# First mixer's query, key and gate projections as seven block products per weight half, with weight sums made beside them

## What is computed

```python
proj = h @ w_in                                  # (512, 1024) @ (1024, 4096)
q, k, v, gate = jnp.split(proj, 4, axis=-1)
...
sc = jnp.einsum('bhqd,bhqnd->bhqn', qb, kg).astype(jnp.float32) * scale
sc = sc + bb.astype(jnp.float32)[None]           # neighbourhood bias, 16 heads
pr = jax.nn.softmax(sc, axis=-1).astype(vg.dtype)
...
return (o * jax.nn.silu(gate)) @ w_out
```

## Time and profile before

| what | us |
|---|---|
| three runs | 1194.61, 1192.61, 1194.82; median 1194.61 |
| profiled execution, device time | 1197.42 |
| span of its trace | 1195.6 |
| busy in the span: PE, DVE, ACT, POOL | 1135.7, 592.3, 507.3, 416.0 |

### The profile page before, as it was taken

How to read it: one execution, slowest core, us unless ns; L and a number is a source line. 1 busy time by engine, 2 the same in 40 slices (tenths; PEclk the granted TensorE clock), 3 DMA queues, 4 the chain that set the end, 5 groups by cost and what they waited for, 6 DMA issues and landing times.

```text
span 1195.6 us, 24300 instructions
## 1 busy us (share of the span) xinstructions
PE 1135.7 (95%) x10103; PEld 952.0 (80%) x10103; DVE 592.3 (50%) x1312; ACT 507.3 (42%) x1025; POOL 416.0 (35%) x363
## 2 busy tenths in 40 slices
PE   3999999999999999899999999988999999999996
PEld 3998888799998998656699998966777887677763
DVE  5000001762427247788623338127875887445656
ACT  4232222973424432488833355243883531122211
POOL 4734574776335445300253334230015341000000
PEclk9999999999999999999999999989999899999999
DMA  7432342323221223200042223342002222100001
GB/s 218 147 98 79 106 115 97 98 69 85 72 86 56 93 85 106 71 1 2 4 139 72 72 71 128 124 137 71 2 2 71 71 91 98 55 27 3 4 2 70
DMA packets 73335, 89.57 MB, mean 75 GB/s; under 512 B 2017, under 2 KB 66666, under 8 KB 73098
## 3 DMA queue, kind: packets, MB, share of 16 engines
q1 hardware_dynamic: 70136, 78.12, 20.3%
q0 software_dynamic: 2416, 8.26, 2.8%
q10 hardware_dynamic: 674, 1.64, 0.5%
HBM read 83.75 MB, written 4.26 MB: 74 GB/s over the span
## 4 chain that ended last, share of the span: by engine, by line
PE 83%; DVE 7%; ACT 5%; POOL 2%; issue 2%; ACTq 1%; DMA 0%; DVEq 0%; POOLq 0%
PE bank L477 77%; PE bank L804 2%; ACT arena L1378 2%; POOL ring_parts L2697 2%; PE bank L714 1%; PE bank L1003 1%; ACT ring_parts L1407 1%; PE bank L569 1%; ACT arena L1494 1%; ACT arena L1759 1%; ACTq L1373 1%; DVE arena L2420 0%; ACT arena L1387 0%; DMA ring<-in_cmp_w_v 0%; POOL arena_parts L2703 0%
## 5 line engine op out<-in xcount | busy, mean ns | idle before, releaser
L2697 POOL TENSOR_TENSOR ring_parts<-ring,ring_parts 128x512 fp32r<-128x512 f32 (+1 forms) x236 | 307.7, 1337 | 435.7 <-ACT ring_parts L1407 344.0
L477 PE MATMUL bank<-ring_parts,arena_parts 128*128 128x256 f32 x1856 | 322.8, 283 | 0.0
L477 PEld LDWEIGHTS bank<-ring_parts,arena_parts 128*128 128x128 f32 x1856 | 272.2, 190 | 2.0 <-DVE stat L2245 1.2
L477 PE MATMUL bank<-hT_parts,ring_parts 128*128 128x512 f32 x704 | 235.2, 396 | 0.0
L477 PE MATMUL bank<-arena_parts,ring_parts 128*128 128x512 f32 x640 | 225.3, 402 | 2.8 <-POOL ring_parts L2697 2.8
L477 PE MATMUL bank<-ring_parts,hT_parts 128*128 128x256 f32 x1024 | 222.9, 285 | 3.8 <-POOL ring_parts L2697 2.9
L1378 ACT ACTIVATE arena<-bank 128x512 f32<-128x512 f32 (+5 forms) x287 | 135.2, 540 | 195.3 <-PE bank L477 191.4
L477 PEld LDWEIGHTS bank<-ring_parts,hT_parts 128*128 128x128 f32 x1024 | 172.2, 192 | 5.0 <-POOL ring_parts L2697 3.7
L477 PE MATMUL bank<-arena 64*64 64x64 f32 (+7 forms) x1904 | 163.0, 316 | 6.8 <-ACT arena L1759 2.3
L477 PEld LDWEIGHTS bank<-hT_parts,ring_parts 128*128 128x128 f32 x704 | 133.4, 190 | 31.3
L477 PEld LDWEIGHTS bank<-arena_parts,ring_parts 128*128 128x128 f32 x640 | 122.9, 192 | 32.1 <-ACT arena L1378 3.0
(11 more groups left out here) (271 smaller groups left out, 1406.5 us busy)
## 6 DMA issues: line engine op xcount, KB each, us to landing
ring<-in_a_w_in SPq DMA_DIRECT2D x16, 1024.0 KB, 5.5
ring<-in_w_in SPq DMA_DIRECT2D x15, 1024.0 KB, 5.5
ring<-in_b_w_in SPq DMA_DIRECT2D x10, 1024.0 KB, 5.0
ring<-in_ple_w_gate SPq DMA_DIRECT2D x8, 1024.0 KB, 5.2
...
```

The costliest lines, as they stand in the source:

```text
L477: return nc.tensor.matmul(o, l, r, start=start, stop=stop)
L2697: nc.gpsimd.tensor_tensor(rounded(r), r, read_back(high_slot(n)[:, o:o + m // 4]), ALU.subtract)\
```

## The change

The four values halves stay as they are. For the twelve others (`SEVEN`, h = 0 to 11) the product is cut into 2 x 2 x 2 blocks (512 rows of k, 128 output features, 256 tokens) and made of seven block products instead of eight, with sums of weight blocks on the left and sums of token blocks on the right.

- **TensorE.** A product (`seventh`, number m = 7h + q) is 4 k x 3 matmuls with 256 moving columns. Products q = 4, 5, 6 go on in banks that hold q = 0, 3, 1, once these have been read.
- **Operands.** Six double places of 128x512 (`operand`, `NOP` = 6) take the weight operands, high and low; they lie in the fourth raw slot and both high slots, and the raw halves turn over three slots. ScalarE writes the high part (`high_operand`), GpSimd the low part of q = 0, 1, 2, 3, 6, VectorE that of q = 4, 5. VectorE makes the four weight sums of a half (`sum_operand`). Operands are prepared five products ahead and wait for the product that frees their place.
- **Tokens.** VectorE makes three sums of token blocks of 128x1024 and one in place, and their low parts, during the values halves. They lie in `x` and in the arena; SyncE loads `x` again behind `AO` 3.
- **Results.** ScalarE copies the first product; VectorE adds the others to it (`second_out`, `third_out`, `last_out`); ScalarE reads the block of q = 4 (`left_out`). Gates: tanh from the copied gate, then `gate_a` on VectorE from two tiles in SBUF.
- **GpSimd.** All low parts of operands stand before head 4's bias. The four quarters of `AO` 0 stand before the biases of heads 8 to 11, those of `AO` 1 before heads 12 to 15. Two small DMAs into `wa` move behind the attention, since `wa` holds a weight sum.

The core of the diff:

```diff
-        AORD = list(range(8, 12)) + list(range(8)) + list(range(12, 16))
+        SEVEN = list(range(8)) + list(range(12, 16))
+        AORD = list(range(8, 12)) + SEVEN
         for n in AORD:
-            half(("A", n), A["a_w_in"][0], n)
...
+        def operand(m):
+            o = HALF * NRAW7 + 2 * 4 * P * ((m + 2) % NOP)
+            return quarter(ring[:, o:o + 4 * P]), quarter(ring[:, o + 4 * P:o + 8 * P])
+        s2_sum = quarter(wa[:, :])
+        h_full, h_low = (v["norm0"].rearrange("p (k t) -> p k t", k=KB) for v in (full, low))
+        x4 = x[:, :, :].rearrange("p i d -> p (i d)")
+        T1, T2, T4 = ((quarter(x4[:, 0:1024]), quarter(x4[:, 3072:4096])),
+                      (quarter(x4[:, 1024:2048]), quarter(area(16384, 1024))),
+                      (quarter(x4[:, 2048:3072]), quarter(area(17408, 1024))))
+        def tokens_of(kh, th):
+            return block4(hT[:, :, :], kh, th, 256), block4(h_low, kh, th, 256)
+        T3 = tokens_of(0, 1)
+        RIGHT = [tokens_of(0, 0), T1, T2, T3, tokens_of(1, 0), T4, tokens_of(1, 1)]
+        def source(m):
+            h, q = divmod(m, 7)
+            return {0: weight_block(h, 0, 0), 1: weight_block(h, 0, 1), 2: s2_sum, 4: weight_block(h, 1, 0),
...
+        LAST_OF = ("1", "6", "6", "7", "11", "21", "12")
+        def free_operand(eng, m):
+            if m < 2:
+                eng.wait_ge(filled, half_last[2] + 1)
+            elif m < NOP:
+                eng.wait_ge(filled, half_last[3] + 1)
+            else:
+                h, q = divmod(m - NOP, 7)
+                eng.wait_ge(filled, J[("A", SEVEN[h], LAST_OF[q])] + 1)
...
+            def seventh(m, b, again=False):
+                h, q = divmod(m, 7)
+                if q in (4, 5):
+                    pe.wait_ge(S("A_low_v"), 2 * h + q - 3)
                 else:
-                    for s in range(2):
-                        fm3(("A", n, s), "a" if n < 8 else "v", ("A", n), s * P, act)
-                used3(("A", n))
+                    pe.wait_ge(S("A_low_g"), 5 * h + min(q, 4) + 1)
+                left, right = (tuple(rounded(v) for v in pair) for pair in (operand(m), RIGHT[q]))
+                def one(a, c, k, st, sp):
+                    return nc.tensor.matmul(b[:, 0:256], left[a][:, k, :], right[c][:, k, :], start=st, stop=sp,
+                                            skip_group_check=again)
+                for k in range(4):
+                    one(0, 0, k, k == 0 and not again, False)
+                    one(0, 1, k, False, False)
+                    ins = one(1, 0, k, False, k == 3)
+                return ins
+            pe.wait_ge(S("A_tlow"), 3)
+            for h, n in enumerate(SEVEN):
+                m = 7 * h
+                b1 = begin(("A", n, "11"), "a", apart=True)
+                also(("A", n, "1"), ("A", n, "11"), "a")
+                end(seventh(m, b1), ("A", n, "1"))
+                b5 = begin(("A", n, "12"), "v", apart=True)
+                seventh(m + 1, b5)
+                b6 = begin(("A", n, "6"), "v", apart=True)
+                end(seventh(m + 2, b6), ("A", n, "6"))
+                b7 = begin(("A", n, "21"), "v", apart=True)
+                also(("A", n, "7"), ("A", n, "21"), "v")
+                if h == 0:
+                    pe.wait_ge(S("A_tlow3"), 1)
+                end(seventh(m + 3, b7), ("A", n, "7"))
+                evacuated(pe, ("A", n, "1"))
+                end(seventh(m + 4, b1, True), ("A", n, "11"))
+                evacuated(pe, ("A", n, "7"))
+                end(seventh(m + 5, b7, True), ("A", n, "21"))
+                pe.wait_ge(S("A_22"), h + 1)
+                end(seventh(m + 6, b5, True), ("A", n, "12"))
...
+            def high_operand(m):
+                h, q = divmod(m, 7)
+                if q in (1, 2, 3, 6):
+                    act.wait_ge(S("A_sum"), 4 * h + min(q, 4))
+                else:
+                    raw_here(act, first7 + h)
+                free_operand(act, m)
+                nc.scalar.activation(rounded(operand(m)[0]), source(m), ACT.Copy).then_inc(S("A_high"), 1)
...
+            def h_block(kh, t):
+                return block4(h_full, kh, t, 256)
+            evacuated(dve, ("norm0", 3, 1))
+            dve.wait_ge(s_wlo, 8)
+            TT(T1[1], h_block(0, 1), h_block(0, 0), ALU.subtract).then_inc(S("A_tsum"), 1)
+            dve.wait_ge(S("A_tsum"), 1)
+            TT(T2[1], h_block(1, 1), T1[1], ALU.subtract).then_inc(S("A_tsum"), 1)
+            dve.wait_ge(S("A_tsum"), 2)
+            TT(T4[1], h_block(1, 0), T2[1], ALU.subtract).then_inc(S("A_tsum"), 1)
+            dve.wait_ge(S("lo_norm0"), 8)
+            TT(h_block(0, 1), h_block(1, 1), h_block(0, 1), ALU.subtract).then_inc(S("A_tsum"), 1)
+            for n, t in enumerate((T1, T2, T4)):
+                dve.wait_ge(S("A_thigh"), n + 1)
...
+            def sum_operand(m):
+                h, q = divmod(m, 7)
+                if q == 1:
+                    raw_here(dve, first7 + h)
+                    s1 = weight_block(h, 0, 1)
+                    TT(s1, s1, weight_block(h, 1, 1), ALU.add).then_inc(S("A_sum"), 1)
+                    dve.wait_ge(S("A_sum"), 4 * h + 1)
+                    if h:
+                        dve.wait_ge(S("A_low_g"), 5 * h - 2)
+                    TT(s2_sum, s1, weight_block(h, 0, 0), ALU.subtract).then_inc(S("A_sum"), 1)
+                if q in (3, 6):
+                    free_operand(dve, m)
+                    dve.wait_ge(S("A_sum"), 4 * h + 2)
+                    TT(operand(m)[1], weight_block(h, 1, int(q == 3)), s2_sum, ALU.subtract).then_inc(S("A_sum"), 1)
+            def low_operand(m):
+                h, q = divmod(m, 7)
+                if q in (4, 5):
+                    dve.wait_ge(S("A_high"), m + 1)
+                    hi, lo = operand(m)
+                    TT(rounded(lo), source(m), read_back(hi), ALU.subtract).then_inc(S("A_low_v"), 1)
+            def second_out(h):
+                n = SEVEN[h]
+                key = ("A", n, "6")
+                b = take(dve, key)
+                evacuated(dve, ("A", n, "1"))
+                give(STT(sums[:, h % 2, 1, :], b[:, 0:256], 0.125 if n < 4 else 1.0, sums[:, h % 2, 0, :],
+                         ALU.mult, ALU.add), key)
+                evacuated(dve, key)
...
+            def third_out(h):
+                n = SEVEN[h]
+                key = ("A", n, "7")
+                b = take(dve, key)
+                u = sums[:, h % 2, 0, :]
+                give(STT(u, b[:, 0:256], 0.125 if n < 4 else 1.0, sums[:, h % 2, 1, :], ALU.mult, ALU.add), key)
+                evacuated(dve, key)
+                out_a(n, 1, bank[slot[("A", n, "12")]], u, 256, 512).then_inc(S("A_22"), 1)
...
+            def gate_a(h, f):
+                n = SEVEN[h]
+                if n >= 12:
+                    k = 2 * (n - 12) + f
+                    dve.wait_ge(S("A_tanh"), 2 * (n - 12) + 2 - f)
+                    STT(G[:, k, :], th[:, f, :], 1.0, G[:, k, :], ALU.add, ALU.mult).then_inc(S("A_gated"), 1)
+            def prepare(m):
+                if m % 7 != 1:
+                    sum_operand(m)
+                if m % 7 == 0:
+                    sum_operand(m + 1)
+                low_operand(m - 1)
...
@@ -2686,22 +2967,26 @@
                 src = bass.AP(scratch.tensor, h * 1024 + 49, [[1, 16], [64, 8], [1, 512]])
                 pool.dma_start(ext[:, h % 2, :], src).then_inc(s_ext[h % 2], 16)
+            def lower_quarter(n, q):
+                pool.wait_ge(s_whi, splits.index(n) + 1)
+                m = halves[n][1][0] * halves[n][1][1] // 4
+                r = raw_slot(n)[:, m * q:m * q + m]
+                nc.gpsimd.tensor_tensor(rounded(r), r, read_back(high_slot(n)[:, m * q:m * q + m]), ALU.subtract)\
...
-            lower(2, HI[("A", 12)])
+            lower(2, 3)
             pool.wait_ge(s_cst, 16)
             mask = C("nbr")
             for h in range(16):
-                if h == 2:
-                    lower(HI[("A", 12)] + 1)
                 if h == 4:
-                    lower(HI[("A", 12)] + 2, HI[("AO", 0)])
+                    for m in range(7 * len(SEVEN)):
+                        if m % 7 not in (4, 5):
+                            pool.wait_ge(S("A_high"), m + 1)
+                            hi, lo = operand(m)
+                            nc.gpsimd.tensor_tensor(rounded(lo), source(m), read_back(hi), ALU.subtract)\
+                                .then_inc(S("A_low_g"), 1)
+                if h >= 8:
+                    lower_quarter(HI[("AO", (h - 8) // 4)], h % 4)
                 pool.wait_ge(s_ext[h % 2], 16 * (h // 2 + 1))
                 if h >= 4:
...
-                    lower(HI[("AO", 1)])
+                    pool.dma_start(wa[0:64, :], A["decay_up_2"][0]).then_inc(s_small, 16)
+                    pool.dma_start(wa[64:128, :], A["iclr_up_2"][0]).then_inc(s_small, 16)
...
+                if prev is not None and first7 <= prev < first7 + len(SEVEN):
```

(16 more changed lines are left out.)

201 lines of the change are left out of this document (152 added, 49 removed).

## The result

| | median us | range | runs |
|---|---|---|---|
| before, beside the change | 1193.92 | 1192.61 to 1194.82 | 4 |
| the change | 1204.26 | 1200.98 to 1205.51 | 4 |

The change makes the kernel slower: ratio 1.0080, 95% interval 1.0062 to 1.0099, 10.3 us. Timed once more beside later experiments it was at 1202.04 (1199.16 to 1206.43) against 1194.25, ratio 1.0063 [1.0041, 1.0084]. The forecast was 1191.8 with a range to 1201. The profiled execution took 1204.83 us and has a span of 1202.6.

What follows compares the result with a forecast made beforehand. TensorE bounds the projections; in the attention TensorE and GpSimd are level. The terms -14.2 + 1.3 + 0.7 + 0.4 + 8.0 + 1.0 give -2.8 us, against the median of 1194.61 a forecast of 1191.8 us, range 1184 to 1201.

Steps and rivals of the forecast that it cites:

- TensorE's work, -14.2: Twelve halves of projections: each falls from 11.12 to 9.94 us at 118 ns per matmul, 14.2 us gained.
- The start, +1.3: Start of the seven products: late first operand and operand 3 cost 1.3 us, between 0 and 3.
- The steady run, +0.7: Products under way: VectorE and GpSimd take turns but stay under 9.94 us per half; 0.7 us lost, from 0 to +13.
- The rival that this sets the pace, at 1203: Products: VectorE and GpSimd taking turns make a half take 10.9 us and TensorE wait, 1203 us; chance 15%.
- The end of the products, +0.4: Last gate: one more VectorE read before tanh, 0.4 us; loads cost nothing, or up to 1 us if they delay bias rows.
- The attention, +8.0: Heads 8 to 15: one more GpSimd subtraction of 1.26 us each makes the attention 8.0 us longer, from 5 to 9.
- The clock in the attention, +1.0: Attention: TensorE's granted clock may fall again, 1.0 us lost, from 0 to 3.4.

Runs made afterwards that it cites:

- n3: The kernel before, with each 512-column matmul in the twelve halves of queries, keys and gates made as two of 256; 1195.18 us.
- k3: The changed kernel with the biases of heads 0 to 3 moved earlier or later on GpSimd, among the values halves and the products; 1204.20 us.
- m2: m1 with ScalarE's high parts of operands 0 and 1 made earlier and GpSimd's first biases and low parts reordered; 1188.35 us.
- a2: The changed kernel as it is, timed and profiled once more; 1202.04 us.
- k2: The changed kernel with the second load of x held until head 15's bias rows have landed; 1198.89 us.
- m1: The changed kernel with the edits of k1 and k2 together; 1189.42 us.
- k1: The changed kernel with AO 0 lowered in one piece before head 4's bias and AO 1 after the attention, instead of quarters; 1193.66 us.

## Why the prediction was wrong

The prediction had the ends of the scale the right way round (TensorE gains in the products, GpSimd loses it in the attention) and missed by 12.5 us. Up to the output projection the forecast was some 3 us earlier than the earlier trace rows and it came 5.6 us later. By its own terms:

- **TensorE's work, -14.2.** The mechanism was right, the size off: 10.08 instead of 9.94 us per half, since I took 118 ns from the values halves; the steady pace of the products is 120.0, as in n3, and why is open. That is 12 x 0.14 = 1.7 us less gain.
- **The start, +1.3. This step failed.** It was a wait of 2.7 and, with it, a clock fall that cost another 2.7 (123.69 us for 1008 matmuls that take 121.0 at 120.0 ns): +5.4. The prediction walked along GpSimd's queue only ("behind the low parts that end at 59.29: 72.5, and 73.8 with the first operand"). It left out that ScalarE's high part of that operand stands behind its last bank read, at 74.36; and it had GpSimd's four heads without waits for their rows, which took 0.85 and 2.10 us, so that both engines were late alike. k3 took the one away and gained 0.5 us; m2 took both away and the wait and the fall were gone, though only 2.0 us of the 5.4 came back: the bank read behind the sums came next.
- **The steady run, +0.7.** It cost nothing: 96 of 96 us. VectorE and GpSimd do take turns (from 86 to 196 us GpSimd's subtractions average 1.40 us, and 1.75 for the one that reads `wa`, instead of 1.26, the second sum on VectorE 1.66 instead of 0.69), but it stays in the slack. The rival that this sets the pace, at 1203, came close to the measured time for a reason that the profile shows wrong. The rule that it leaned on, of the Trainium skill (SBUF — State Buffer, "SBUF: two separate sides" and "Who interferes with whom"), is borne out in that the two exclude each other and again not in the length: k3's longest, at 1.78 us, waited 1.09 where the subtraction is 1.26.
- **The end of the products, +0.4 and "cost nothing" for the second load of x. This step failed too.** It said of the loads "up to 1 us". Measured: 3.80 us idle ahead of head 6 (4.96 in a2), 3.0 us of length in k2, 2.8 in m1. I had compared the load with its reader, 50 us later, and not with the DMA that is in flight beside it and that GpSimd, without slack from there on, waits for.
- **The attention, +8.0.** The mechanism was right and the size near. Between k2 and m1, which differ in the quarters alone, the length differs by 8.9 us, where the prediction had 8.9 for head 15's bias and 8.0 for what follows; from the change to k1 it is 9.2.
- **The clock in the attention, +1.0.** It was 1.00 throughout; the fall came at the start of the products instead. In k1, m1 and m2 there was one of 0.72 to 0.76 from 204 to 210.

Added up from the profiles: 1.7 less gain, 4.1 at the start, 0.7 less in the steady run, and 3.5 for the length (66.25 against 53.3 + 0.4 + 8.0 + 1.0 = 62.7), together 8.6. The prediction's -2.8 becomes +5.8, and the output projection moved by 5.6. The rest up to the medians' 8 to 10 us lies behind it, where the runs with the seven products have 3 to 4 us more than those without; the prediction had no term for that, and its cause stays open.
